# One expert per round of SyncE's loop, with the ring slot taken from a register

## The chip, the cores and the metric

The kernel runs on one core of a Trainium2 chip. The metric is the device time of one execution in microseconds. The median of three runs before the change is 1522.88 us (1520.92 to 1523.11). The profile comes from one further execution, which took 1525.86 us.

## The reference

The program is one layer of a diffusion backbone on 512 latent tokens of width 1024 with a context of 256 tokens: an adaLN-modulated RMSNorm, a mixer of two head groups (Fourier mixing and a bidirectional RG-LRU), an output projection with a gated residual, and then a mixture of 32 clamped SwiGLU experts, of which each token takes 4. The experts take four fifths of the time, and the change is in their part:

```
logits = hf @ w_router + b_router                 # (512, 32)
top_val, top_idx = lax.top_k(logits, 4); gates = softmax(top_val)
for each block of rows that chose expert e:
    gu  = xb @ w_gate_up[e] + b_gate_up[e]        # 1024 -> 2048
    gt  = min(gu[:, :1024], 7); up = clip(gu[:, 1024:], -7, 7)
    act = (up + 1) * gt * sigmoid(1.702 * gt)
    out = act @ w_down[e] + b_down[e]             # 1024 -> 1024
    y[token] += gate * out
```

All of it is float32. The weights of one expert are 8 MB (w_gate_up) and 4 MB (w_down), and every expert's weights are read from HBM once.

## The kernel before, in words

The part ahead of the experts (about 320 us) is not touched. For the experts the routed rows are cut into items of 64 rows, all of one expert; an expert has one item or more, and with these inputs there are 45 items. The order of the experts is worked out on the chip and lies in the table `order_i`; `before_i[i]` tells the last item ahead of the expert that is i-th in that order.

TensorE, VectorE, ScalarE and GpSimd each run a loop over the items (L1507, L1181, L774, L576), with as many rounds as there could be items at most (63) and an `If` that passes over those that don't exist. An item needs its expert's 12 chunks of weights: chunks 0 to 7 are gate/up, 8 to 11 down, 1 MB each. VectorE (L1030, chunks 0 to 5, 8 and 9) and ScalarE (L765, chunks 6, 7, 10 and 11) copy each chunk from a ring in SBUF to one of four windows, from which TensorE multiplies (L1480 gate/up, L1492 down). The ring has NR = 16 slots of one chunk, and the chunk c of the p-th expert lies in slot (12 p + c) mod 16. The copying engines already take that slot from a register (`ring_chunk`, L328).

SyncE fills the ring. `load_chunk` (L313 to L322) issues two transfers of 512 KB for a gate/up chunk (L319) and one of 1 MB for a down chunk (L322). `load_expert` (L438 to L448) does the 12 chunks of an expert: for each it waits until the chunk that had the slot has been moved by its last item (L445), waits until the transfer of that chunk number for the expert before has landed (L447), and issues. The expert's number comes from `order_i` by a register load (L439), so the source of a transfer is an address in a register, while its slot is a constant: since 4 experts are 48 chunks, the slots repeat with PERIOD = 4 experts. The first expert's chunks are issued one by one ahead of the tables; experts 1 to 3 are written out; and a loop of 7 rounds (L456) holds four experts each. `last_item_ahead_of` (L435, L436) is one register load. After the loop SyncE waits for the ring's last readers and brings back what the output norm needs.

The order of work around the change is set by semaphores alone: SyncE's program is one sequence, and its transfers go to one hardware queue (q1); the only other users of DMA in this part are GpSimd's gathers and scatters (q0) and the fetching of instructions.

Of the kernel before, what the change touches and what calls it, by code (L numbers as in the profile page):

```python
# [25 lines left out]
NE, TOPK = 32, 4  # L26
# [7 lines left out]
HF = FF // 2  # L34
# [4 lines left out]
CK = 2  # L39
NCH = 12  # L40
NW = 4
NR = 16
PERIOD = 4
OUT_OF_RANGE = 4096
KB = 1024

# [53 lines left out]
def build(nc, x, ctx, w_mod, b_mod, w_in, w_fourier, rg_w_a, rg_w_x, w_out, w_router, b_router,  # L100
# [5 lines left out]
    with ExitStack() as stack:  # L106
# [11 lines left out]
        def at(name, shape, off, dt=F32):  # L118
            return nc.alloc_sbuf_tensor_at(name, shape, dt, offset=off)
# [12 lines left out]
        def sem(name):  # L132
            return stack.enter_context(nc.semaphore(name))
# [80 lines left out]
        ring = at("ring", [P, NR, CK, 2, HF], SLOT[0])  # L214
# [74 lines left out]
        wgu_v = w_gate_up.rearrange("e (k p) n -> e p k n", p=P)  # L289
        wd_v = w_down.rearrange("e (k p) n -> e p k n", p=P)  # L290
# [19 lines left out]
        w_ld = [sem(f"w_loaded_{c}") for c in range(NCH)]  # L310


        def load_chunk(sp, c, e, p):  # L313
            h, k = c // 4, c % 4 * CK
            s = (NCH * p + c) % NR
            if h < 2:
                for g in range(2):
                    n0 = g * FF + h * HF
                    sp.dma_start(ring[:, s, :, g, :], wgu_v[e, :, k:k + CK, n0:n0 + HF]).then_inc(w_ld[c], 16)  # L319
            else:  # L320
                k = (c - 8) * CK
                sp.dma_start(ring[:, s, :, :, :].rearrange("p k g n -> p k (g n)"), wd_v[e, :, k:k + CK, :]).then_inc(w_ld[c], 16)  # L322

        def landed_at(c):
            return 32 if c < 8 else 16
# [6 lines left out]
        def wait_moved(eng, c, item):  # L332
            if c in BY_DVE:
                eng.wait_ge(S["moved_by_dve"], len(BY_DVE) * item + BY_DVE.index(c) + 1)
            else:
                eng.wait_ge(S["moved_by_act"], len(BY_ACT) * item + BY_ACT.index(c) + 1)
# [28 lines left out]
        def _(sp):  # L365
# [42 lines left out]

            sp.wait_ge(S["pf_done"], TL)
            load_chunk(sp, 6, 0, 0)  # L410
            load_chunk(sp, 7, 0, 0)
            sp.wait_ge(S["ssr_done"], 1)
            load(bias_raw[:, :], bias_rows, "ld_bias")
            sp.wait_ge(S["pr_done"], TL)
            for c in range(4):
                load_chunk(sp, c, 0, 0)
# [16 lines left out]
            n = sp.value_load(n_items[0:1, 0:1], min_val=NE, max_val=NI)  # L433

            def last_item_ahead_of(i):  # L435
                return sp.value_load(before_i[0:1, bass.ds(i, 1)], min_val=0, max_val=NI)  # L436

            def load_expert(i, p, ahead, ahead_of_last):  # L438
                e = sp.value_load(order_i[0:1, bass.ds(i, 1)], min_val=0, max_val=NE - 1)  # L439
                for c in range(NCH):  # L440
                    if c >= NR - NCH:
                        wait_moved(sp, c - (NR - NCH), ahead)
                    elif ahead_of_last is not None:
                        wait_moved(sp, c + 2 * NCH - NR, ahead_of_last)
                    sp.nop(nofuse=True)  # L445
                    sp.wait_ge(w_ld[c], landed_at(c) * i)
                    sp.nop(nofuse=True)  # L447
                    load_chunk(sp, c, e, p)  # L448

            sp.wait_ge(S["stored"], 16 * TL)  # L450
            last = None
            for p in range(1, PERIOD):
                ahead = last_item_ahead_of(p)
                load_expert(p, p, ahead, last)
                last = ahead
            with sp.Fori(1, NE // PERIOD) as r:  # L456
                last = last_item_ahead_of(r * PERIOD - 1)
                for p in range(PERIOD):
                    ahead = last_item_ahead_of(r * PERIOD + p)
                    load_expert(r * PERIOD + p, p, ahead, last)  # L460
                    last = ahead
            last = last_item_ahead_of(NE - 1)
            wait_moved(sp, 9, last)
            sp.nop(nofuse=True)
# [1106 lines left out]
```

## Time and profile before

| | us |
|---|---|
| median of 3 runs | 1522.88 |
| the profiled execution | 1525.86 |
| its span, first to last instruction | 1524.0 |
| TensorE busy | 1346.3 |
| VectorE busy | 910.6 |
| ScalarE busy | 647.3 |
| GpSimd busy | 254.8 |
| share of the 16 DMA engines that queue q1 took | 81.7% |

Busy times are sums over one engine, and engines run side by side, so they don't add up to the span. SyncE does not show in the table at all: issuing transfers, waits and register instructions are not counted as busy. In the rows its work has the name SPq, and a transfer's issue (DMA_DIRECT2D) is shown as long as SyncE was held by it, which includes the time in which the queue would take no more. "DMA share" is the mean busy share of the 16 DMA engines; because packets overlap a little it reads up to about 1.05 when they are full.

### The profile page before, as it was taken

To read this page: it belongs to the slowest core of one execution; us is meant where nothing else is said; L and a number is where in the kernel's file an instruction comes from. 1 tells how busy PE (TensorE), PEld (TensorE's weight loads), DVE (VectorE), ACT (ScalarE), POOL (GpSimd) and SP (SyncE) were. 2 spreads that over 40 slices of the span, in tenths; PEclk is the share of its full clock that TensorE was granted. 3 is DMA by queue.
4 is the path that set the end of the run, shared out by engine and by line. 5 is a ranking of instruction groups with operands and counts; after the bars stand their busy time and mean duration, and the time that the engine had idled before them with its cause. 6 is when DMAs were issued, how large, how long until landed. Compare 5 with 4: busy or idle time off the path is not lost.

```text
span 1524.0 us, 25174 instructions
## 1 busy us (share of the span) xinstructions
PE 1346.3 (88%) x6259; PEld 540.7 (35%) x6259; DVE 910.6 (60%) x1451; ACT 647.3 (42%) x720; POOL 254.8 (17%) x156
## 2 busy tenths in 40 slices
PE   4798999579999998999889879999999989979981
PEld 2586558423333332333223223333333323223320
DVE  3999786856556654555556445565565455545555
ACT  3433453234444444444354334544444434334442
POOL 1741143211011111011111101110111101101111
PEclk9799989779999999999999999999999999999995
DMA  9666222779999999599999993799999999999993
GB/s 378 230 217 219 84 111 76 276 243 371 349 384 341 373 385 387 196 376 382 380 379 383 377 377 81 246 383 322 379 358 380 381 381 375 380 372 379 368 386 124
DMA packets 208310, 478.84 MB, mean 314 GB/s; under 512 B 18561, under 2 KB 19073, under 8 KB 207233
## 3 DMA queue, kind: packets, MB, share of 16 engines
q1 hardware_dynamic: 197426, 459.44, 81.7%
q0 software_dynamic: 10832, 18.90, 5.6%
q14 instruction: 43, 0.35, 0.1%
q8 instruction: 9, 0.15, 0.0%
HBM read 465.16 MB, written 20.45 MB: 319 GB/s over the span
## 4 chain that ended last, share of the span: by engine, by line
PE 33%; SPq 30%; DVE 13%; DMA 11%; issue 10%; ACT 2%; DVEq 0%; POOL 0%; ACTq 0%; POOLq 0%
SPq L319 23%; PE ps L1480 18%; DMA ring<-in_w_down 7%; PE ps L1492 7%; SPq L322 5%; DVE bc L877 4%; DMA wm<-in_w_mod 2%; DVE window L1030 2%; ACT window L765 1%; PE ps L1472 1%; PE ps L1358 1%; PE ps L1382 1%; PE ps L1383 1%; PE ps L1384 1%; DMA ring<-in_w_gate_up 1%
## 5 line engine op out<-in xcount | busy, mean ns | idle before, releaser
L1480 PE MATMUL ps<-window,xT 128*64 128x512 f32 x2880 | 649.8, 599 | 38.9 <-DVE window L1030 23.4
L1030 DVE COPY window<-ring 128x2048 f32 (+1 forms) x364 | 445.0, 1228 | 343.3 <-DMA ring<-in_w_gate_up 109.2
L1492 PE MATMUL ps<-window,aT 128*64 128x512 f32 x1440 | 342.1, 604 | 32.1 <-DVE window L1030 21.9
L765 ACT ACTIVATE window<-ring 128x2048 f32 x180 | 339.9, 1908 | 58.1 <-DMA ring<-in_w_down 45.8
L1480 PEld LDWEIGHTS ps<-window,xT 128*64 128x64 f32 x2880 | 196.0, 137 | 422.5 <-issue 344.2
L759 ACT ACTIVATE sg<-gb 128x256 f32<-128x256 f32 x90 | 37.5, 416 | 435.8 <-DVE gb L1168 435.8
L572 POOL DMA_INDIRECT y_rows<-osb,idx_c x46 | 77.7, 1690 | 635.7 <-ACT osb L755 620.9
L1492 PEld LDWEIGHTS ps<-window,aT 128*64 128x64 f32 x1440 | 90.7, 136 | 189.3 <-issue 133.3
L559 POOL DMA_INDIRECT xg<-h_rows,idx_n x46 | 67.7, 1472 | 429.0 <-DVE idx_n L1060 429.0
L1168 DVE TENSOR_SCALAR gb<-ps 128x256 f32<-128x256 f32 x90 | 38.2, 424 | 162.3 <-PE ps L1480 161.4
L755 ACT ACTIVATE osb<-ps,gate_c 128x512 f32<-128x512 f32 x46 | 31.7, 688 | 119.7 <-PE ps L1492 118.8
L777 ACT ACT_TABLE_LOAD x45 | 57.7, 1283 | 13.1 <-issue 13.1
L1472 PE MATMUL ps<-bias_w,pick 128*128 128x512 f32 x135 | 56.0, 469 | 0.7 <-ACT xT L748 0.7
L1472 PEld LDWEIGHTS ps<-bias_w,pick 128*128 128x128 f32 x135 | 22.0, 189 | 73.1 <-issue 72.2
L1298 PE MATMUL ps<-hT_l_hi,win_hi 128*128 128x512 f32 x96 | 39.0, 406 | 7.2 <-DVE hT_l_lo L864 7.2
L1502 PEld LDWEIGHTS ps<-csb,ab 128*128 128x128 f32 x180 | 18.1, 141 | 76.7 <-DVE ab L1175 46.6
L748 ACT ACTIVATE xT<-ps 128x512 f32<-128x512 f32 x46 | 27.4, 597 | 39.6 <-PE ps L1461 39.6
L1502 PE MATMUL ps<-csb,ab 128*128 128x128 f32 x180 | 39.5, 301 | 3.1 <-DVE ab L1175 3.1
L1461 PEld LDWEIGHTS ps<-csb,xg 64*128 64x128 f32 x368 | 27.1, 142 | 41.8 <-issue 41.8
L1175 DVE TENSOR_TENSOR ab<-ub,sg 128x256 f32<-128x256 f32 x90 | 38.3, 425 | 3.1
L1172 DVE SCALAR_TENSOR_TENSOR ub<-ub,gb 128x256 f32<-128x256 f32 x90 | 38.3, 425 | 3.1
L1299 PE MATMUL ps<-hT_l_lo,win_hi 128*128 128x512 f32 x96 | 38.4, 400 | 0.0
(279 smaller groups left out, 1182.7 us busy)
## 6 DMA issues: line engine op xcount, KB each, us to landing
ring<-in_w_gate_up SPq DMA_DIRECT2D x512, 512.0 KB
ring<-in_w_down SPq DMA_DIRECT2D x128, 1024.0 KB
wm<-in_w_mod SPq DMA_DIRECT2D x4, 2048.0 KB, 21.7
wm_a<-in_w_mod SPq DMA_DIRECT2D x4, 2048.0 KB, 9.1
wm_b<-in_w_mod SPq DMA_DIRECT2D x4, 2048.0 KB, 8.6
win<-in_w_in SPq DMA_DIRECT2D x3, 2048.0 KB, 20.2
x_in<-in_x SPq DMA_DIRECT2D x1, 2048.0 KB, 10.6
wo_f<-in_w_out SPq DMA_DIRECT2D x1, 2048.0 KB, 7.4
```

Of the source, the lines that this page charges most:

```text
L319: sp.dma_start(ring[:, s, :, g, :], wgu_v[e, :, k:k + CK, n0:n0 + HF]).then_inc(w_ld[c], 16)
L322: sp.dma_start(ring[:, s, :, :, :].rearrange("p k g n -> p k (g n)"), wd_v[e, :, k:k + CK, :]).then_inc(w_ld[c], 16)
L559: pool.indirect_dma_start(xg[0:M, :], None, h_dram, bass.IndirectOffsetOnAxis(ap=idx_n[0:M, 0:1], axis=0), bounds_check=last_row, oob_is_e ...
L572: pool.indirect_dma_start(y_dram, bass.IndirectOffsetOnAxis(ap=idx_c[:, 0:1], axis=0), osb[:, :], None, bounds_check=last_part, oob_is_err ...
L765: A(window[c % NW][:, :, :, :], ring_chunk(c, p), ACT.Copy).then_inc(S["moved_by_act"], 1)
L777: A(table_kept[:, :], ones[:, 0:1], ACT.Sigmoid)
L877: ins = V.scalar_tensor_tensor(Z, W[:, k, :], csil[:, k, 0:1], Z, ALU.mult, ALU.add)
L1030: V.tensor_copy(window[c % NW][:, :, :, :], ring_chunk(c, p)).then_inc(S["moved_by_dve"], 1)
L1472: return MMUL(ps[:, bank, :], pick[:, :], bias_w[:, bank * CH:(bank + 1) * CH], start=True, stop=False)
L1480: last = MMUL(ps[M * j:M * (j + 1), h, :].rearrange("m (g n) -> m g n", g=2), xT[:, k, :], window[c % NW][:, k % CK, :, j * GW:(j + 1) * G ...
L1492: last = MMUL(ps[M * y:M * (y + 1), 2, :], aT[:, h, i, M * j:M * (j + 1)], window[c % NW][:, k % CK, y, :], start=False, stop=(h == 1 and ...
L1502: last = nc.tensor.transpose(ps[:, 3, h * GW + i * P:h * GW + (i + 1) * P], ab[:, i * P:(i + 1) * P], ident)
```

## The change

SyncE's loop holds one expert and runs 30 times (experts 2 to 31); expert 1 stays written out ahead of it. The slot in `load_chunk` is no longer a Python number but an expression of the expert's index, evaluated in registers, so both ends of a transfer are now addresses from registers (in the written-out chunks the index is a Python number, and the slot stays a constant). `before_i` is read twice per expert where it was read 5 times for 4 experts. `PERIOD` goes. The transfers, their order, sizes and shapes, and the values waited for are the same.

```diff
         def load_chunk(sp, c, e, p):
             h, k = c // 4, c % 4 * CK
-            s = (NCH * p + c) % NR
+            s = bass.ds((p * NCH + c) & (NR - 1), 1)
             if h < 2:
                 for g in range(2):
                     n0 = g * FF + h * HF
-                    sp.dma_start(ring[:, s, :, g, :], wgu_v[e, :, k:k + CK, n0:n0 + HF]).then_inc(w_ld[c], 16)
+                    sp.dma_start(ring[:, s, :, g, :].rearrange("p s k n -> p (s k) n"), wgu_v[e, :, k:k + CK, n0:n0 + HF]).then_inc(w_ld[c], 16)
             else:
                 k = (c - 8) * CK
-                sp.dma_start(ring[:, s, :, :, :].rearrange("p k g n -> p k (g n)"), wd_v[e, :, k:k + CK, :]).then_inc(w_ld[c], 16)
+                sp.dma_start(ring[:, s, :, :, :].rearrange("p s k g n -> p (s k) (g n)"), wd_v[e, :, k:k + CK, :]).then_inc(w_ld[c], 16)
...
-            def load_expert(i, p, ahead, ahead_of_last):
+            def load_expert(i, ahead, ahead_of_last):
...
-                    load_chunk(sp, c, e, p)
+                    load_chunk(sp, c, e, i)
...
-            last = None
-            for p in range(1, PERIOD):
-                ahead = last_item_ahead_of(p)
-                load_expert(p, p, ahead, last)
-                last = ahead
-            with sp.Fori(1, NE // PERIOD) as r:
-                last = last_item_ahead_of(r * PERIOD - 1)
-                for p in range(PERIOD):
-                    ahead = last_item_ahead_of(r * PERIOD + p)
-                    load_expert(r * PERIOD + p, p, ahead, last)
-                    last = ahead
+            load_expert(1, last_item_ahead_of(1), None)
+            with sp.Fori(2, NE) as i:
+                last = last_item_ahead_of(i - 1)
+                load_expert(i, last_item_ahead_of(i), last)
```

## Rows read from the trace of the kernel before

**Rows 1.** The page: DMA share by slices, then the chain by line.

```profile
DMA  9666222779999999599999993799999999999993
SPq L319 23%; PE ps L1480 18%; DMA ring<-in_w_down 7%; PE ps L1492 7%; SPq L322 5%; DVE bc L877 4%; DMA wm<-in_w_mod 2%; DVE window L1030 2%; ACT window L765 1%; PE ps L1472 1%; PE ps L1358 1%; PE ps L1382 1%; PE ps L1383 1%; PE ps L1384 1%; DMA ring<-in_w_gate_up 1%
```

**Rows 2.** Windows: stretch and length, PE, PEld, DVE, ACT, POOL busy, clock, DMA share, GB/s.

```profile
345.00:600.00 255.00, 248.16 (x1187) 82.75 (x1186) 146.27 (x242) 117.86 (x123) 33.87 (x21) 1.00 1.02 369
920.00:1135.00 215.00, 211.96 (x1015) 71.27 (x1017) 127.24 (x215) 103.55 (x107) 28.73 (x18) 1.00 0.83 290
```

**Rows 3.** Windows, each two experts of SyncE's issuing, without and with a back edge.

```profile
759.10:828.90 69.80, 64.26 (x307) 21.30 (x309) 39.85 (x69) 33.44 (x34) 7.37 (x5) 1.00 1.05 381
828.90:898.90 70.00, 58.57 (x272) 18.13 (x270) 32.07 (x53) 24.79 (x26) 8.60 (x5) 1.00 1.04 378
...
1225.90:1297.20 71.30, 67.04 (x313) 22.22 (x315) 40.48 (x70) 34.66 (x35) 7.95 (x6) 0.98 1.05 378
1297.20:1367.80 70.60, 58.80 (x266) 18.07 (x264) 31.56 (x52) 23.57 (x26) 7.37 (x5) 0.98 1.04 374
```

**Rows 4.** Waits of SyncE: total, times, longest; whole span, then 1125 to 1480 us.

```profile
SPq L445 <- DVE window L1030: 161.9, 47, 47.4
...
SPq L445 <- DVE window L1030: 1.9, 1, 1.9
```

**Rows 5.** Chain around a back edge of SyncE's loop: start, length, what.

```profile
564.94 0.06 SPq L456
565.00 5.42 issue
570.42 0.07 SPq L456
...
570.53 0.28 SPq L436
...
571.21 0.27 SPq L436
...
573.34 0.03 SPq L319
...
573.40 0.37 SPq L319
```

**Rows 6.** DMA queues: one round (721.5 to 862 us), then 330 to 1500, then 0 to 330.

```profile
q14 instruction: 5, 0.04, 0.1%
...
q14 instruction: 36, 0.29, 0.1%
...
q8 instruction: 9, 0.15, 0.2%
```

**Rows 7.** Windows over the back edge at 862 us and what follows it.

```profile
862.10:867.30 5.20, 2.75 (x14) 0.88 (x14) 4.00 (x12) 2.33 (x2) 0.00 (x0) 1.00 1.03 414
...
867.30:882.00 14.70, 9.83 (x49) 3.15 (x47) 4.25 (x7) 5.52 (x6) 0.98 (x1) 1.00 1.03 358
882.00:892.00 10.00, 8.70 (x42) 2.47 (x40) 3.68 (x3) 3.84 (x5) 2.62 (x1) 1.00 1.02 368
...
1346.00:1356.00 10.00, 10.00 (x46) 3.36 (x46) 1.97 (x3) 6.62 (x7) 0.73 (x1) 0.83 1.00 355
```

**Rows 8.** Lines L319 (window 325 to 358 us, then whole) and L1030: duration min/median/max.

```profile
L319 SPq DMA_DIRECT2D ring<-in_w_gate_up x16: 372/373/543, 326.3 to 346.8; - x16
...
L319 SPq DMA_DIRECT2D ring<-in_w_gate_up x512: 209/917/5602, 242.7 to 1463.2; - x171
...
L1030 DVEq ALU_OP  x675: 40/45/57, 323.0 to 1490.4; - x169
L1030 DVEq FUSED_REGOPS  x405: 46/57/64, 322.9 to 1490.5; - x135
```

**Rows 9.** Chain through VectorE's back edge in rounds with no item.

```profile
1498.88 0.06 DVEq L1181
1498.94 0.23 issue
```

More of the change, by code:

```diff
@@ L42 @@
 NR = 16
-PERIOD = 4
 OUT_OF_RANGE = 4096
```

## The prediction

> **What bounds the kernel now.** I read the page first, and in it the slices of the DMA share beside the chain by line [rows 1]. From slice 8 on the DMA engines are full except at slices 16 and 24 to 25, and the chain gives 23% to SyncE's issuing of gate/up transfers (L319) and 18% to TensorE's gate/up products (L1480). That reads as two regimes, and SyncE has a large share of one, so the first question is whether SyncE or the DMA behind it is the limit there.
>
> The windows by stretch separate the regimes. From 345 to 600 us and from 920 to 1135 us TensorE is busy 97% and 99% of the time [rows 2]: experts with several items, whose weights arrive faster than they are used. The ring fills, and the waits of SyncE show it standing at a slot's wait for up to 47.4 us [rows 4]. Between 600 and 915 us (less some 27 us of a full ring in slice 16) and from 1135 to 1480 us the DMA share is 1.04 to 1.05, and TensorE has gaps [rows 3]. There 25.2 MB, two experts, take 69.8 to 71.3 us, 35 us for each. These stretches sum to 315 - 27 + 345 = 633 us, or 18 experts.
>
> In the second regime SyncE doesn't wait for slots (1.9 us from 1125 to 1480 us [rows 4]); it is held inside the issue. The line's rows tell why: where the queue has room an issue takes 0.37 us, over the whole span the median is 0.92 us and the longest 5.6 us [rows 8]. The queue takes no more; SyncE is only where that shows. So 35 us of an expert are DMA time, and SyncE's own work must be counted apart.
>
> **SyncE's own time for an expert.** 20 transfers at 0.373 us [rows 8] are 7.5 us. The rest of an expert are some 86 small instructions by the code: two ahead of each transfer (40), three per chunk for its two waits (36), and about ten at the top. Small ones start 0.06 to 0.07 us apart (573.34 to 573.40 [rows 5]); that makes 6.0 us. A register load makes 0.68 us from one to the next (570.53 to 571.21 [rows 5]), so 2.25 of them add about 1.5 us. The sum is 15 us of the 35.
>
> **What is removed.** Between the branch of L456 and the first instruction of the next round lie 5.42 us in which SyncE waits for nothing that the profile names [rows 5]. Queue q14 carries five packets of 8 KB in one round (0.04 MB) and 36 from 330 us on [rows 6]: SyncE's instructions are fetched anew in every round, and at the branch back it stands until the first packet is in. The loop has 6 such edges taken, 32 us in all. The new loop holds one expert. Its instructions are 106 now plus what is added, some 170 where the old round has about 430. The nearest row for whether such a loop still fetches is TensorE's: q8 has 9 packets ahead of 330 us and none after, while TensorE's loop runs 45 items [rows 6]; its body is the longer one, 1,187 matmuls in 255 us [rows 2], 24.3 us an item, so 113 matmuls with as many weight loads. I take it that the new loop stays loaded, and that an edge then costs what VectorE's does, 0.06 + 0.23 = 0.3 us [rows 9].
>
> What is the removal worth on the end? The window over the edge at 862 us has a DMA share of 1.03 and 414 GB/s while SyncE stands still: the transfers already queued cover it [rows 7]. The next two windows have 1.03 and 1.02 against 1.05 elsewhere, a loss of 0.02/1.05 x 14.7 + 0.03/1.05 x 10 = 0.6 us. The worst window after another edge, that of 1330 us, has 1.00, 0.5 us in ten. Two experts with an edge take 70.0 and 70.6 us, two without 69.8 and 71.3 [rows 3]: no difference. Of the six edges one (1054 us) lies in the first regime; for the other five I take 0.26 us each, 1.3 us gained. The bounds are 0 and 5 x 0.65 = 3.2 us.
>
> **What is added.** No row of before shows a transfer with its slot in a register, but VectorE's copies read the same expression: 1,080 register instructions over 360 copies, three for each address [rows 8]. Three on 20 transfers are 60, at 0.07 us 4.2 us per expert. If only the last step is made per transfer it is 20 x 0.07 = 1.4 us; with a fourth (the source has two) 5.6 us. I take 4.2, from the nearest row. The issue itself may change as well: the source's address already comes from a register, and the issue takes 0.37 us with it, so I take no change; the bounds are 0 and the 0.92 us median in place of 0.37, which would add 11 us per expert. One `before_i` load more in three experts of four is 0.75 x 0.68 = 0.5 us, the more frequent edge 0.23 us, and the lost fetches give back 6 x 5.3 / 30 = 1.1 us. SyncE's own time goes from 15 to 19 us (16 to 21 by the first bounds), and 35 us are there. The cover is the wait for the queue; it is gone only if SyncE's time passes 35 us.
>
> Two places have no such cover. When a full ring opens, the transfer of the freed slot goes out 0.2 us (three instructions) later; this counts once for each passage from the first regime to the second, some 4 times, 0.8 us (0 to 1.1). In the first regime nothing is owed: a ring of 16 chunks lies ahead of TensorE. The output's loads behind the loop (L467) start when the last transfers have been issued, and those are paced by DMA.
>
> **The sum.** 1525.9 us (the profiled execution) - 1.3 + 0.8 = 1525.4 us, which is 0.5 us below; on the median of the runs, 1522.9, that is 1522.4 us. All that SyncE does besides, +4 us on each of 30 experts, and -32 us of standing still, lies behind the DMA engines. The likeliest case's own range is 1520 to 1525 us.
>
> The Trainium skill ("Runtime: NRT & Kernel Launch", section "Instruction fetch mechanics") has a rule against this change: a taken branch whose target isn't in the current window of two pages forces a fetch of the target before execution goes on. The trace agrees for the old loop, which stands 5.42 us. For the new loop the answer depends on the page, which it gives as 16 KiB, 256 instructions, where this trace shows packets of 8 KB on q14. By the larger page a body of 170 would mostly stay; by the smaller one every edge would be a fetch. The next paragraph prices that.
>
> **Rivals.** First: the new loop still fetches at its edge. Then SyncE stands 5.3 us 29 times instead of 6, 35 us after each other instead of 140. SyncE's need per expert is 19 + 5.3 = 24 us, still under 35, but the low backlog that follows an edge comes 18 times: 18 x 0.26 = 4.7 us, less the 1.3 of today, +3.4, and with the 0.8 of the openings +4.2: 1527 us. With the worst edge's 0.65 it is 11.7 - 1.3 + 0.8 = +11: 1534 us. For it: a packet of q14 holds about a hundred instructions (430 over four or five packets), the body is longer than that, and a round of four experts is seen to fetch. Against it: TensorE's loop, whose q8 is silent. It is slower than before by my bound if an edge costs over 0.19 us in lost DMA time: 18 x 0.19 = 3.5 = 3.0 + 1.3 - 0.8.
>
> Second, on the slow side too: the address arithmetic or the issue with two register addresses is dearer than I take it, so that SyncE becomes the limit. It decides from 16 us more per expert, 0.8 us on each of 20 transfers. At 1.0 us it would be 20 - 16 = 4 us on 18 experts, +72 us: 1595 us. For it: no row shows the form. Against it: an issue with a register source takes 0.37 us, and three small instructions 0.2.
>
> Third, faster: the standing still does cost what the chain says. The chain has 5.42 us of "issue" there [rows 5], and five such edges in the second regime are 27 us: 1496 us. A weaker form, in which the whole bound of 0.65 us is saved and nothing is lost at the openings, gives -3.2: 1519.7 us. Against it: 414 GB/s in the very window [rows 7], and pairs of experts that don't differ [rows 3].
>
> Fourth, the change may not do what it says, in that the expression is worked out for each chunk but the fetches remain in part (a body over three blocks of 8 KB, say). That is the first rival with fewer edges, between it and mine.
>
> **How the numbers follow.** What a measurement of this kernel can tell from no change is about 0.2%, 3.0 us: below 1519.8 us is faster, above 1525.9 us slower. My case 0.72; the first rival with the fourth 0.17; the second 0.03; the third 0.08. Of my case 0.03 falls below 1519.8 (the edges' upper bound) and 0.03 above 1525.9; of the first rival 0.11 lies above 1525.9 and 0.06 within. Faster: 0.08 + 0.03 = 0.11. Slower: 0.11 + 0.03 + 0.03 = 0.17. The same: 0.72. The range goes from 1518.5, which leaves out the third rival's strong form, to 1529, which takes in the first rival at its likeliest size.
>
> **What would show it.** Right: no 5 us of "issue" behind L456's branch, q14 all but silent after some 345 us; L319 with three more register instructions per transfer; issues in the second regime with a lower median than 0.92 us, since SyncE comes later to a queue that is full anyway; a DMA share of 1.04 to 1.05 in the same stretches, and the same 35 us per expert. First rival: 29 gaps of 5 us and about 90 packets on q14, with windows under 1.00 after each. Second: a DMA share under 1.0 in the second regime. Third: a share above 1.05, or pairs of experts below 69 us. My forecast is wrong if the time leaves 1520 to 1525 us, and its reason is wrong if the time holds but the DMA share in these stretches falls.

## The result: 9 us faster, and the profile after

The changed kernel took 1513.81 us (median of 7 runs, 1512.79 to 1517.02), the kernel before 1522.88 us beside it (7 runs, 1519.69 to 1523.95): a ratio of 0.9949 [0.9938, 0.9959]. That is 9.1 us less where 0.5 us less was forecast, outside 1520 to 1525 us and below the range. The profiled execution took 1514.07 us, 11.8 us below that of before.

The page of the changed kernel: its span, the DMA share by slices, the queues that carry instructions (packets, MB, share), and the chain by line.

```profile
span 1512.2 us, 26040 instructions
...
DMA  9666222769999999699999993699999999999993
...
q8 instruction: 9, 0.15, 0.0%
q14 instruction: 9, 0.07, 0.0%
...
SPq L318 22%; PE ps L1472 18%; DMA ring<-in_w_down 9%; PE ps L1484 7%; SPq L321 4%; DVE bc L869 4%; DVE window L1022 2%; DMA wm<-in_w_mod 2%; ACT window L757 1%; PE ps L1464 1%; PE ps L1350 1%; PE ps L1374 1%; DVE cv L885 1%; PE ps L1375 1%; PE ps L1376 1%
```

L319 and L322 are now L318 and L321, L1480 is L1472. The picture is that of [rows 1]: the chain's share of SyncE's gate/up issue has gone from 23% to 22%, and no slice of the DMA share tells where 9 us were. Queue q14 does tell something. From 345 to 1480 us the changed kernel has

```profile
q14 instruction: 1, 0.01, 0.0%
```

where the kernel before has 35 packets in that stretch (36 from 330 us on [rows 6]):

```profile
q14 instruction: 35, 0.29, 0.1%
```

The loop stays loaded. At a back edge the chain shows nothing longer than 0.23 us between the branch's instructions and the next round (start, length, what):

```profile
859.31 0.67 SPq L321
859.98 0.04 issue
860.03 0.04 SPq L451
860.07 0.04 issue
860.11 0.04 SPq L451
860.15 0.23 issue
860.38 0.06 SPq L451
860.44 0.04 issue
860.48 0.27 SPq L435
```

against 5.42 us [rows 5]. The gate/up issue line in full (duration in ns, minimum/median/maximum):

```profile
L318 SPq DMA_DIRECT2D ring<-in_w_gate_up x512: 4/823/3948, 241.1 to 1453.0; - x171
L318 SPq FUSED_REGOPS  x496: 2/64/200, 324.2 to 1452.8; - x166
L318 SPq MOVE ring<-in_w_gate_up x496: 2/29/38, 324.8 to 1452.9; - x166
L318 SPq ALU_OP  x480: 1/37/236, 358.3 to 1451.8; - x160
```

The longest issue was 5.6 us and is 3.9 us; the median fell from 0.92 to 0.82 us [rows 8]. The body of an expert has 136 SyncE instructions in the trace, where it had 106: 30 more, one and a half for each transfer, not three.

**Where the time came from.** The windows of the changed kernel over the same work as [rows 2, 3] (stretch and length, PE, PEld, DVE, ACT, POOL busy, clock, DMA share, GB/s):

```profile
345.00:600.00 255.00, 248.37 (x1186) 82.51 (x1182) 145.93 (x242) 116.56 (x122) 33.74 (x21) 1.00 1.02 368
920.00:1133.00 213.00, 210.00 (x1007) 70.42 (x1003) 125.76 (x214) 102.39 (x105) 27.13 (x17) 1.00 0.83 295
756.70:826.50 69.80, 64.80 (x313) 21.36 (x311) 39.85 (x69) 34.45 (x35) 7.76 (x6) 1.00 1.05 381
826.50:895.10 68.60, 58.00 (x270) 18.04 (x268) 32.00 (x52) 23.75 (x26) 8.84 (x5) 1.00 1.05 385
1220.60:1290.90 70.30, 65.42 (x307) 21.71 (x305) 39.54 (x68) 33.73 (x35) 7.36 (x5) 0.98 1.05 378
1290.90:1359.70 68.80, 60.08 (x274) 18.78 (x270) 32.34 (x54) 24.47 (x26) 7.47 (x5) 0.98 1.05 383
1359.70:1428.50 68.80, 64.45 (x309) 21.33 (x307) 39.75 (x68) 34.22 (x35) 7.36 (x5) 1.00 1.05 382
```

The first regime, in which TensorE is the limit, is as it was. In the second, in which the DMA engines are full, the two pairs of experts that held a back edge went from 70.0 to 68.6 us and from 70.6 to 68.8 us, with 385 and 383 GB/s for 378 and 374. Those without an edge went from 69.8 to 69.8 and from 71.3 to 70.3. The last pair, which has no edge either, had taken 69.7 us before:

```profile
1367.80:1437.50 69.70, 64.29 (x307) 21.30 (x309) 39.95 (x69) 33.42 (x34) 7.37 (x5) 1.00 1.04 373
```

The share of 1.05 for 1.04 is one unit of its last digit; the GB/s, 9 more in 373, is the column that tells. The gain goes with the packets that q14 carried before: the two pairs with an edge held four each (840, 866, 870 and 898 us; 1308, 1334, 1339 and 1367 us) and became 1.4 and 1.8 us shorter, and the three without held one each (797, 1264 and 1405 us) and became 0, 1.0 and 0.9 us shorter.

The same can be read from TensorE's items, timed from the start of their bias products in the two profiled executions: an item that isn't short of weights takes 24.3 us in both. The items short of weights took 8.2 us less in sum, and no others changed; 1.5 us came before the first item and 2.0 us after the last, where nothing was changed. That is the 11.8 us.

### The profile page after: what moved, and what is told of

Its sections match the earlier page's. It is cut to its first block, busy times and chain, and to the rows that moved or that the text cites. A ratio compares the mean times of both kernels' runs of the same rounds, so it can differ in the third digit from the quotient of the medians.

```text
span 1512.2 us, 26040 instructions
## 1 busy us (share of the span) xinstructions
PE 1343.9 (89%) x6259; PEld 539.5 (36%) x6259; DVE 907.9 (60%) x1451; ACT 646.9 (43%) x720; POOL 257.6 (17%) x156
## 4 chain that ended last, share of the span: by engine, by line
PE 33%; SPq 29%; DVE 13%; DMA 12%; issue 8%; ACT 3%; DVEq 1%; POOL 0%; ACTq 0%; POOLq 0%
SPq L318 22%; PE ps L1472 18%; DMA ring<-in_w_down 9%; PE ps L1484 7%; SPq L321 4%; DVE bc L869 4%; DVE window L1022 2%; DMA wm<-in_w_mod 2%; ACT window L757 1%; PE ps L1464 1%; PE ps L1350 1%; PE ps L1374 1%; DVE cv L885 1%; PE ps L1375 1%; PE ps L1376 1%
## 5 line engine op out<-in xcount | busy, mean ns | idle before, releaser
L1472 PE MATMUL ps<-window,xT 128*64 128x512 f32 x2880 | 647.4, 598 | 33.5 <-DVE window L1022 21.0
L1472 PEld LDWEIGHTS ps<-window,xT 128*64 128x64 f32 x2880 | 195.9, 137 | 414.9 <-issue 345.2
L485 POOL TENSOR_TENSOR win_lo<-win,win_hi 128x1024 fp32r<-128x1024 f32 x12 | 31.4, 2622 | 45.4 <-ACT win_hi L619 45.3
```

The costliest lines, as they stand in the source:

```text
L1472: last = MMUL(ps[M * j:M * (j + 1), h, :].rearrange("m (g n) -> m g n", g=2), xT[:, k, :], window[c % NW][:, k % CK, :, j * GW:(j + 1) * G ...
```

## The experiments

Each time is a median of 4 to 11 runs, and the ratio, with its 95% interval, is against the kernel before, measured beside it (1522.78, 1524.11, 1523.42 and 1523.44 us in the four groups of runs). Three theories were at hand: (A) SyncE's standing still costs more than its cover suggests; (B) the fetches of instructions cost, by delaying DMA, whether SyncE stands or not; (C) something else of the new loop, such as its register slots, helps.

**Loops taken apart.** u1_unrolled: no loop and constant slots.

```
+            for p in range(1, NE):       # all experts written out
+                load_expert(p, p, ahead, last)   # slot (NCH*p + c) % NR, a constant
```

> The kernel before with all 31 experts of SyncE's sequence written out: no branch back, and the slot a constant as before. Theory A (the gain is the standing still of 5.3 us at the branch, which costs the DMA queue about 1 to 2 us each in the second regime): no gap of 5 us on SyncE, and the time of the changed kernel, 1512 to 1515 us. Theory B (the gain comes from how the register arithmetic spaces SyncE's issues): the time of the kernel before, 1521 to 1524 us, since the spacing is the old one.

1516.55 us, 0.9953 [0.9940, 0.9966]: it gives 6.2 us without a branch and without a register in the slot, with 24 packets of q14 from 345 to 1480 us. C is not needed.

u2_four_reg: the old loop with the new slots.

```
-            s = (NCH * p + c) % NR
+            s = bass.ds((p * NCH + c) & (NR - 1), 1)
             ...
             with sp.Fori(1, NE // 4) as r:       # four experts a round, as before
```

> Four experts per round as before, with the slot from a register as in the changed kernel. Theory A: the gaps of 5.3 us stay at 6 edges, so the time of before, 1521 to 1524 us. Theory B: 1512 to 1515 us.

1528.68 us, 1.0029 [1.0016, 1.0042]. The six halts are there, of 5.2 to 5.5 us. Its round has 526 instructions where the old one has 430, and q14 carries 42 packets where it carried 35. Of the two parts of the change, the register slots in the old loop are a loss, 5.9 us by the medians, and the shorter loop is all of the gain.

u4_two_reg: the same text with two experts in a round.

> Two experts per round (about 270 instructions of SyncE), slot from a register, 15 rounds. If such a body stays loaded: no gap at the edge, queue q14 silent in the loop, 1512 to 1515 us. If it does not: 14 gaps of 5.3 us, about 9 of them in the second regime; by theory A at 1.3 us each 1522 to 1528 us.

1517.58 us, 0.9957 [0.9945, 0.9969]: 266 instructions in a round stay loaded (2 packets of q14). Against u2_four_reg 11.1 us. A halt and a fetch still come together here.

w4_three: three experts in a round, 396 instructions.

> Three experts per round, slots from registers, nothing else added: some 400 instructions, ten rounds. If they stay loaded, 1513 to 1517 us and q14 silent in the loop. If not: 9 halts of 5.3 us, some 5 or 6 in the second regime, and by the run with four per round 1523 to 1529 us.

1531.33 us, 1.0047 [1.0031, 1.0063]. It fetches again, 48 packets from 345 us on, with nine halts of 5.2 to 6.0 us. More halts, more packets, a longer time.

**The halt by itself.** u3_wait8: the changed kernel, which fetches nothing, with eight more loads of `before_i` in each round.

```
             with sp.Fori(2, NE) as i:
+                for _ in range(8):
+                    last_item_ahead_of(i - 1)
```

> The changed kernel with eight more register loads at the head of every round, some 5.5 us of SyncE's time 30 times, with nothing fetched. Theory A, with 1.3 us lost per edge in the second regime: 18 experts there, so +15 to +25 us on the changed kernel, 1529 to 1539 us. If only the fetch as such costs (its packets, or a stall that the loads don't imitate): 1513 to 1516 us. The predicted 0.26 us per edge would give 1518 us.

1519.15 us, 0.9972 [0.9961, 0.9983]. From the branch to the first issue of a round SyncE takes 7.4 us here and 2.8 us in the changed kernel, so the halt is 4.6 us (an expected load was 0.68 us, and one takes 0.55). On each of 30 experts it cost 3.5 to 5.3 us in all, where A, at 1.3 us for each expert of the second regime, expected 15 to 25. The 1518 us that 0.26 us per edge would give is near, but not for its reason: by the table below the loss lies where the second regime opens.

v1_same: the changed kernel once more, as the ground for the three that follow.

> The changed kernel once more, as the measure for the three others of this job: 1512 to 1516 us by every theory.

1514.29 us, 0.9938 [0.9925, 0.9952].

v2_every4: the halt of the kernel before, near its length and at its places, with nothing fetched.

```
             with sp.Fori(2, NE) as i:
+                with sp.If((i & 3) == 0):
+                    for _ in range(8):
+                        last_item_ahead_of(i)
```

> The changed kernel with eight more register loads (5.5 us of SyncE's time, nothing fetched) ahead of each expert whose index divides by 4: the place and length of the standing still of the kernel before, without its fetches. Theory S (a rare halt of SyncE costs more than an even one): the time of the kernel before, 1520 to 1523 us. Theory F (the cost is tied to the fetch of instructions, by its packets or by how the engine halts): 1514 to 1516 us, 0.3 us for each of 5 halts.

1515.40 us, 0.9946 [0.9933, 0.9960]: 1.1 us above v1_same for seven halts, of which five lie in the second regime, 0.2 us for each of these. The intervals of the two runs overlap, so it may be nothing. Against the kernel before it is still 8.7 us less. This is the experiment that rules A out. Its windows over the pairs that hold a halt:

```profile
826.70:894.70 68.00, 58.19 (x270) 18.02 (x268) 32.43 (x54) 23.55 (x26) 7.92 (x5) 1.00 1.05 386
1291.00:1359.60 68.60, 57.72 (x268) 17.79 (x264) 32.36 (x53) 23.30 (x24) 7.32 (x5) 1.00 1.05 383
```

and those of u2_four_reg, which stands about as long there, but fetches:

```profile
831.50:900.80 69.30, 60.42 (x268) 18.47 (x264) 31.08 (x50) 24.14 (x26) 7.99 (x5) 0.95 1.04 376
1299.50:1370.70 71.20, 58.15 (x262) 17.66 (x258) 31.10 (x50) 23.32 (x24) 7.77 (x5) 0.98 1.04 369
```

With about the same halt it is 386 and 383 GB/s without a fetch, 376 and 369 with it. The halts can be read in the chains. Of u2_four_reg:

```profile
863.94 0.38 SPq L321
...
864.50 5.28 issue
...
869.89 0.28 SPq L435
```

and of v2_every4, where one of the eight loads follows the other (0.27 us and 0.15 us, and small pieces, 0.55 us each):

```profile
859.85 0.27 SPq L435
860.12 0.03 issue
860.15 0.15 SPq L435
860.31 0.05 issue
```

From the branch to the next issue SyncE takes 7.7 us in these rounds of v2_every4, 7.7 to 7.9 us in the kernel before, and 2.8 us in the changed one.

v3_wait16: sixteen loads in each round, which take 8.9 us (11.7 us from the branch to the next issue, less 2.8).

> Sixteen more register loads in every round, 10.9 us of SyncE's time for each expert. SyncE's own need becomes 19 + 11 = 30 us of 35. If the queue covers halts as with eight loads (0.3 us each there): +10 to +15 us on the changed kernel. If it runs dry, 1.5 to 3 us in each of 18 experts: +27 to +54 us.

1541.58 us, 1.0117 [1.0101, 1.0132]: 27 us on v1_same. That reads as if the cover had an end between 4.6 and 8.9 us per expert, but TensorE's items put 20.7 us of it at the three openings of the second regime and only 3.0 us later in it. The windows of v3_wait16 and then of the changed kernel over most of the second regime:

```profile
700.00:900.00 200.00, 175.45 (x823) 56.10 (x819) 99.59 (x168) 83.69 (x87) 23.86 (x15) 1.00 1.03 373
1190.00:1470.00 280.00, 248.84 (x1165) 79.73 (x1165) 147.26 (x246) 119.25 (x124) 33.03 (x20) 1.00 1.04 377
...
700.00:900.00 200.00, 178.82 (x837) 56.85 (x831) 102.91 (x177) 85.09 (x87) 24.78 (x15) 1.00 1.05 383
1190.00:1470.00 280.00, 254.97 (x1185) 82.38 (x1181) 147.28 (x251) 120.81 (x124) 33.13 (x21) 0.99 1.05 383
```

Once a backlog has formed the queue still makes SyncE wait: from 1230 to 1450 us the median gate/up issue takes 0.66 us, against 0.37 us where there is room [rows 8].

**Fetches without halts.** Four kernels put in instructions that do nothing. v4_skip had 450 in a branch never taken; w1_one_nop, w2_two_nop and w3_unr_nop had 140 for each expert, in the changed kernel, in two experts a round and in the unrolled one.

```
+                with sp.If(i == NE):
+                    for _ in range(450):
+                        sp.nop(nofuse=True)
```

> The changed kernel with 450 instructions behind each expert that are jumped over and never run, so that the loop no longer stays loaded: by the trace of before, two fetch halts of 5.3 us in every round, the forward jump's and the branch's back, 10.7 us per expert with two or more packets on q14. Theory S: the time of the kernel with sixteen loads, within 4 us. Theory F: slower than that one by 10 us or more.

> The changed kernel with 140 empty instructions of SyncE ahead of each expert (some 276 instructions a round, 7 to 9 us of SyncE's time per expert). Two experts of about that length in all stayed loaded before, so q14 should stay silent. It is the measure for the next two. By the run with eight loads, 0.2 to 0.4 us per expert in the second regime: 1519 to 1526 us by every theory.

> The same with two experts per round, so some 550 instructions that don't stay loaded: 14 halts for a fetch, about 9 of them in the second regime, and some five packets on q14 per round, 75 in all. Theory S (only SyncE's time counts): within 4 us of the run with one expert per round and 140 empty instructions. Theory F (a fetch costs about 1.5 us per edge in the second regime, besides SyncE's halt): +10 to +18 us on that run.

> All experts written out, slots constant, the same 140 empty instructions ahead of each: about 60 packets on q14 and no halt. If the packets themselves cost (0.1 to 0.25 us each): +3 to +15 us on the run with one expert per round. If only a fetch that SyncE waits for costs: the same as that run or up to 4 us less, since the register arithmetic is gone.

None of them shows (the rounds of w1_one_nop and w2_two_nop still had 136 and 266 instructions, and in all four q14 had the packets of the kernel without them), so their expectations weren't tested, and the four are repetitions: 1513.89 us, 0.9937 [0.9924, 0.9951] and 1515.57 us, 0.9947 [0.9930, 0.9965] for the changed kernel; 1516.98 us, 0.9952 [0.9936, 0.9968] for two a round; 1516.25 us, 0.9950 [0.9935, 0.9965] unrolled.

Waits that are already fulfilled do stand in the trace, each with its empty instruction as one of some 0.06 us.

```
                 e = sp.value_load(order_i[0:1, bass.ds(i, 1)], min_val=0, max_val=NE - 1)
+                for _ in range(100):             # 130 in x3_unr_wait
+                    sp.wait_ge(S["ld_cst"], 16)
+                    sp.nop(nofuse=True)
```

x1_one_wait: in the changed kernel, 236 instructions a round.

> The changed kernel with 100 waits of SyncE that are long fulfilled ahead of each expert (about 235 instructions a round, some 6 us of SyncE's time). No fetch, so one DMA engine lags the others at a down chunk by less than 1.5 us. 1515 to 1520 us by both theories; it is the measure for the next.

1522.32 us, 0.9993 [0.9984, 1.0002]. It doesn't fetch, and still costs 8 us on the changed kernel, for 5.8 us more of SyncE's time per expert. That was above its expectation of 1515 to 1520 us; the next section has where most of it lies.

x2_two_wait: two experts a round with the same waits, some 466 instructions.

> The same 100 waits per expert with two experts per round, about 465 instructions, too long to stay loaded: 14 halts for a fetch, about 9 in the second regime. Theory S (SyncE's time alone): within 4 us of the run with one expert per round. Theory E (a fetch at a halt delays one of the 16 DMA engines, and the queue and every chunk wait for that one): 1.5 to 2.3 us for each of 9, so +13 to +21 us, and the last of the 16 completions of a down chunk 3 us or more behind the 15th.

1578.93 us, 1.0377 [1.0362, 1.0392], 56.6 us on x1_one_wait, with 14 halts of 5.7 to 6.4 us. From 345 to 1480 us it has

```profile
q14 instruction: 85, 0.70, 0.2%
```

That is far above what was expected. SyncE's own work is some 27 us of the expert here (7.5 of issues, 16.5 of small instructions, 3 of halt), and by the table of the next section most of the time is lost where SyncE has no backlog. The run mixes the fetch with SyncE's slowness and settles nothing by itself.

x3_unr_wait: unrolled, no branch and no halt. From 345 to 1480 us it has

```profile
q14 instruction: 54, 0.44, 0.1%
```

> All experts written out, constant slots, 130 fulfilled waits ahead of each: some 55 packets on q14 where the run written out without them had 25, and no halt. If each packet costs one DMA engine its 0.34 us, and 35 of them fall in the second regime: up to 8 us on the run written out, 1517 to 1525 us, with the last completion 2 us or more behind the 15th. If only a fetch that SyncE waits for matters: 1515 to 1519 us.

1540.27 us, 1.0111 [1.0096, 1.0126]: 18 us on x1_one_wait and 24 us on u1_unrolled. It has no register slots and 130 waits for 100, which nearly evens out: the trace has 7,276 SyncE instructions here and 7,368 in x1_one_wait. No instruction of SyncE stands still for a fetch here, and the time goes up with the packets all the same. B says so, A doesn't; B's expectation had its size too small (1517 to 1525 us).

## What a fetch does, and where it costs

Each ring transfer adds 16 to its semaphore, in 16 steps as its parts end on the DMA engines. From the recorded steps I took, for each down chunk from 700 to 915 us and from 1190 us to the end (some 60 in each kernel), the time from the 15th step to the last. The other columns come from TensorE's items: how much longer than in the changed kernel the items at the three openings of the second regime took (items 10, 11, 16, 17, 34, 35), and those later in it (21, 22, 39, 40). Items are counted from 0. All of it is worked out from one profiled execution each. Between the four executions of the changed kernel, repetitions included, the openings differ by up to 2.5 us and the later items by up to 1.2 us.

```
                 q14 packets   last step behind the 15th   openings   later
                 345-1480 us   mean, max (us)              (us)       (us)
changed               1        0.73, 2.19                    0          0
v1_same (again)       1        0.27, 1.46                   -2.5       +0.2
v4_skip (again)       1        0.41, 1.73                   -0.4       -1.0
w1_one_nop (again)    1        0.59, 1.54                   -0.6       +0.1
v2_every4             2        0.51, 1.60                   -1.0       +0.1
u3_wait8              2        0.32, 1.64                   +4.6        0.0
x1_one_wait           2        0.47, 2.08                   +5.0       +0.8
v3_wait16             2        0.38, 1.64                  +20.7       +3.0
u4_two_reg            2        0.56, 2.38                   +0.7       +0.3
u1_unrolled          24        1.13, 2.77                   -1.6       +1.7
w3_unr_nop (again)   24        0.81, 2.27                    0.0       +2.1
before               35        2.81, 5.59                   +2.2       +5.5
u2_four_reg          42        3.37, 6.70                   +6.1       +6.4
w4_three             48        2.91, 6.14                   +8.2       +5.5
x3_unr_wait          54        3.02, 7.28                  +12.5      +10.0
x2_two_wait          85        3.28, 6.92                  +40.7      +13.5
```

Two things cost. Kernels that hardly fetch lose next to nothing later in the second regime with up to 5.8 us more of SyncE's time per expert (u3_wait8, x1_one_wait), and 3.0 us with 8.9 us more (v3_wait16); their last step comes 0.3 to 0.7 us behind the 15th in all cases. Those that fetch 35 packets or more have it 2.8 to 3.4 us behind, and lose 5.5 us and more there. One of the 16 parts is late, and a chunk is usable only when the last is in.

The delay adds up. The down chunk of index 10, of the kernel before, was late by 0.2 us at 1134 us, then by 0.7, 2.6, 1.5, 1.9 and 2.1 us up to 1310 us, 3.1 us at 1347 us (the edge was at 1330), and 4.9, 4.3 and 5.6 us at 1381, 1415 and 1451 us. No edge comes after 1330 us, but packets of the same round do, at 1339, 1367, 1405 and 1448 us. The changed kernel has 0.8, 0.8, 0.5 and 0.2 us in the last four places, v2_every4 0.5 to 0.9. The lateness falls back, from 2.1 to 0.1 us and from 2.9 to 0.5 us, only at 667 and 989 us, behind a time in which the ring was full. So the mean of 2.8 us is not what one fetch does. By the median of an expert's four down chunks the last step of the kernel before moved from 0.2 to 2.1, from 0.2 to 2.9 and from 0.7 to 4.7 us in the three stretches of the second regime, 8.6 us in sum, over 21 packets: 0.4 us for each, where a packet took 0.34 us, and where TensorE's items lost 8.2 us. This is an estimate from one execution; the same count gives 0.4 us for u2_four_reg, 0.15 for u1_unrolled, 0.6 for x3_unr_wait, 0.3 for w4_three and 0.1 for x2_two_wait, and in the last two the items lost far more than the last step moved.

At the openings, SyncE comes from a slot's wait to an empty queue, and its own time is on the path until a backlog has formed. Added time costs there with or without a fetch: 4.6 us for u3_wait8, 5.0 us for x1_one_wait, which is most of its miss, and 20.7 us for v3_wait16. A late part in these items stands in the same column.

I read this as: a fetch runs on the same DMA engines as the weights, delays one of them, and the queue takes new transfers only as that one allows. Shown are the packets, the late last step, the lower GB/s and the price of it. Not shown is that it is the fetch's own engine that is late, since the trace doesn't number the engines. Nor is it settled why a packet moves the last step by less than its own time in the unrolled kernel and by nearly twice that in x3_unr_wait; why the register slots cost more with the fetch (u2_four_reg 6 us above the kernel before, with 7 packets more) than without (u4_two_reg within 4 us of the changed kernel); and how much of the 2 us between the unrolled and the changed kernel is their 24 packets.

No kernel of the study is below the changed one, whose four measurements lie at 1513.8 to 1515.6 us.

## Why the prediction was wrong, step by step

- **The step that failed** is the worth of the removal: "for the other five I take 0.26 us each, 1.3 us gained", with an upper bound of 0.65 us each, 3.2 us in all. The prediction counted 36 packets of instructions and gave them no price. Removing loop and fetch gave 6.2 us unrolled and 9.1 us in this change: for five edges 1.2 to 1.8 us each. Against u4_two_reg and w2_two_nop, loops that fetch cost 2.2 us (u2_four_reg) and 2.4 us (w4_three) per halt in the second regime. That is a price per halt in name only: about half of the packets come between the halts.
- **What held of it**: the halt is covered by what is queued. v2_every4 gives 0.2 us for a halt of its length, near the 0.26 and not clear of nothing. I had priced the standing still and named it the price of the edge; the fetch's effect on the transfers was not in the sum as a term of its own.
- **Why the rows misled.** "Two experts with an edge take 70.0 and 70.6 us, two without 69.8 and 71.3: no difference" took the two kinds of pair to be alike but for the edge. They aren't: in the changed kernel, where none has an edge, the same pairs take 68.6 and 68.8 us against 69.8 and 70.3. The pairs with an edge would have been the shorter ones, and their four packets took that away. The pairs without an edge weren't free of fetches either, and were late already. And the price was read from the DMA share, a mean over 16 engines with two digits, in which one late engine is a 16th. The column beside it had it: from 381 to 378 and from 378 to 374 GB/s in [rows 3], where the changed kernel goes from 381 to 385 and from 378 to 383. So had the completions of the kernel before, with their 2.8 us.
- **The loop stays loaded**: right, and the first rival is out. One packet of q14, edges without a 5 us gap. In the Trainium skill ("Runtime: NRT & Kernel Launch", section "Instruction fetch mechanics") the window is two pages; rounds of 136, 236 and 266 instructions stayed loaded here and rounds of 396 and more were fetched anew. By the 256 instructions that the Trainium skill gives for a page, two pages would hold 512; rounds of 396 and 430 didn't stay. The prediction's other case, in which packets of 8 KB make every edge of the new loop a fetch, didn't come true either. The same section calls the crossing of a page while running on "mostly hidden". For SyncE's own time x3_unr_wait agrees, where it never stands for a fetch; for the kernel's time it doesn't, by 18 us for 54 packets.
- **The register arithmetic**: 30 instructions per expert, not 60; about 2 us, nearer to the lower bound of 1.4 us than to the 4.2 us taken. What it costs by itself in the changed kernel no run shows.
- **The issue's own time, and SyncE as the limit**: no change of kind. The transfers stayed under the wait for the queue, and the second rival fell. The 16 us more from which SyncE would be the limit were not reached by any run: v3_wait16, with 8.9 us more, still waits for the queue, and loses its 27 us mostly at the openings.
- **The openings**, +0.8 us: the place is right and the size too small. The prediction charged the three instructions ahead of one transfer; u3_wait8 and x1_one_wait lose 1.5 and 1.7 us on average at each of three openings for 4.6 and 5.8 us more of SyncE's time per expert, v3_wait16 6.9 us for 8.9 us. SyncE's time for most of an expert is on the path there. In the changed kernel the openings didn't lose 0.8 us but gained 2.2, which is within what two executions differ by.
- **The third rival** had the right sign and, between its two forms (1519.7 and 1496 us), the right neighbourhood. That its strong and weak form enclose the result is luck. One of its signs, "pairs of experts below 69 us", came true at 68.6 and 68.8 us; the other, a share above 1.05, did not. Its reason, that the standing still costs what the chain says, is refuted by v2_every4.

## What to carry to other kernels

A queue of instruction packets that wasn't silent in a DMA-bound stretch was a cost on the transfers here, whether or not the engine stood still for it: count its packets per round, and keep the loop that issues the transfers short enough that they vanish. To price a halt, put the same halt in without the fetch; and for a comparison within one trace, make sure that the neighbour would be alike without the event, and isn't still carrying its effect. In the mean share over 16 engines the late part was nearly invisible here: look at the last of a transfer's completions, or at GB/s.

## What of the hardware was not expected

- Halts of the engine that issues all transfers, 7.7 us from branch to next issue in place of 2.8, cost 0.2 us each or nothing (v2_every4).
- The last of a transfer's 16 steps lay 2.8 us behind the 15th, and up to 5.6 us, in a kernel with 35 packets of instructions in 1135 us, and 0.3 to 0.7 us in kernels with one or two. It grew from packet to packet, by some 0.4 us each in the kernel before, and fell back only where the ring had filled.
- 54 packets read in sequence, with no halt, cost 18 us (x3_unr_wait against x1_one_wait).
- A packet of q14 is 8 KB, and in the two unrolled kernels, u1_unrolled and x3_unr_wait, the trace shows one for each 129 of SyncE's instructions.
